# 32 expert slots shared by two requests, with experts 8 to 31 loaded in the order of a list sorted on the chip

## What is computed

```python
g_idx = argmax(h @ rg_w + rg_b)                       # one of 4 groups of 8 experts
e_sel = (h @ re_w + re_b) of that group               # 8 logits
top_p, top_i = lax.top_k(softmax(e_sel), 2)           # two experts of the group per token
top_w = g_w * top_p / sum(top_p)
hid = silu(h @ w_gate[e]) * (h @ w_up[e]); hid *= combine
y   = sum over e of hid @ w_down[e]
x   = layer_norm(alpha * x + g2 * y)
```

## Time and profile before

| | |
|---|---|
| median of 3 runs | 1063.39 us (1060.44 to 1066.7) |
| span of the profiled execution | 1059.0 us; the page gives no other time for this execution |
| TensorE matmul busy | 957.8 us, 90% of the span |
| VectorE, ScalarE, GpSimd busy | 323.2, 230.0, 36.1 us |
| transfers | 324.60 MB, mean 307 GB/s |
| mean granted TensorE clock | 0.977 of 2.4 GHz |

### The profile page before, as it was taken

One profiled execution on the slowest core, in us unless ns is written; L12 is line 12 of the kernel. 1 busy time (PEld: TensorE's weight loads), 2 busy tenths in 40 slices (PEclk: granted clock), 3 DMA queues, 4 the chain that ended last, 5 costly groups with the idle time before them and its releaser, 6 DMA issues.

```text
span 1059.0 us, 15641 instructions
## 1 busy us (share of the span) xinstructions
PE 957.8 (90%) x6820; PEld 584.3 (55%) x6820; DVE 323.2 (31%) x744; ACT 230.0 (22%) x475; POOL 36.1 (3%) x54
## 2 busy tenths in 40 slices
PE   4999899998998999987979998999998999999695
PEld 1787758776843434324338886687885343432431
DVE  2112323122662212112171232331266331211216
ACT  2102313300143213111131032241014321211111
POOL 0200000010001000000010000000000200000000
PEclk9899999999999999998989999999999999999898
DMA  9948864496658999999798206766466699999981
GB/s 381 409 164 320 361 234 174 170 313 274 282 195 360 399 431 428 430 421 425 299 374 348 108 34 244 306 273 215 162 252 258 273 432 427 427 432 425 424 329 51
DMA packets 38526, 324.60 MB, mean 307 GB/s; under 512 B 4920, under 2 KB 5048, under 8 KB 9392
## 3 DMA queue, kind: packets, MB, share of 16 engines
q1 hardware_dynamic: 34816, 313.02, 72.5%
q0 software_dynamic: 3200, 9.09, 2.7%
q10 hardware_dynamic: 432, 1.39, 0.3%
HBM read 321.05 MB, written 2.42 MB: 305 GB/s over the span
## 4 chain that ended last, share of the span: by engine, by line
PE 83%; ACT 5%; DVE 5%; DMA 4%; issue 3%; SPq 0%; DVEq 0%; ACTq 0%
PE ps L804 16%; PE ps L853 11%; PE ps L699 9%; PE ps L725 6%; PE ps L999 5%; PE ps L913 5%; PE ps L985 5%; PE ps L817 5%; DMA dense<-in_w_ada 4%; PE ps L628 3%; PE ps L863 3%; PE ps L649 2%; PE ps L950 2%; PE ps L669 2%; PE ps L940 2%
## 5 line engine op out<-in xcount | busy, mean ns | idle before, releaser
L804 PE MATMUL ps<-expert_gate_up,gathered_prompt 128*32 128x512 f32 x768 | 170.7, 598 | 4.2 <-ACT gathered_sample L1180 2.3
L804 PE MATMUL ps<-expert_gate_up,gathered_sample 128*32 128x512 f32 x768 | 170.7, 598 | 0.0
L853 PE MATMUL ps<-expert_down,hiddenT 128*32 128x512 f32 x1024 | 118.1, 596 | 9.7 <-ACT gathered_sample L1180 4.6
L699 PE MATMUL ps<-hT,dense 128*128 128x256 f32 x512 | 114.2, 381 | 0.0
L804 PEld LDWEIGHTS ps<-expert_gate_up,gathered_prompt 128*32 128x32 f32 x768 | 48.6, 111 | 114.2 <-issue 111.5
L699 PEld LDWEIGHTS ps<-hT,dense 128*128 128x128 f32 x512 | 96.1, 190 | 15.4 <-issue 2.5
L1595 DVE SCALAR_TENSOR_TENSOR y_lo<-ps,slot_weight,y_hi 128x512 fp32r<-128x512 f32 x64 | 48.1, 751 | 117.3 <-ACT y_hi L1214 117.2
L853 PEld LDWEIGHTS ps<-expert_down,hiddenT 128*32 128x32 f32 x1024 | 31.6, 109 | 76.2 <-issue 59.8
L628 PE MATMUL ps<-dense,cond 128*32 128x256 f32 x768 | 53.2, 406 | 17.0 <-ACT cond L1236 11.7
L725 PE MATMUL ps<-dense,hT 128*128 128x256 f32 (+1 forms) x320 | 66.9, 372 | 1.7 <-ACT hT L1137 1.7
L1578 DVE TENSOR_TENSOR hidden<-hidden,ps 128x256 f32<-128x256 f32 x32 | 13.4, 420 | 179.5 <-ACT hidden L1196 179.4
(11 more groups left out here) (218 smaller groups left out, 1129.4 us busy)
## 6 DMA issues: line engine op xcount, KB each, us to landing
expert_gate_up<-in_w_gu SPq DMA_DIRECT2D x64, 2048.0 KB, 17.2
expert_down<-in_w_dn SPq DMA_DIRECT2D x64, 1024.0 KB, 12.0
dense<-in_w_ada SPq DMA_DIRECT2D x48, 1024.0 KB, 9.1
dense<-in_w_in SPq DMA_DIRECT2D x28, 1024.0 KB, 10.4
dense<-in_w_o SPq DMA_DIRECT2D x8, 1024.0 KB, 6.1
dense<-in_w_out SPq DMA_DIRECT2D x8, 1024.0 KB, 4.9
dense<-in_w_c SPq DMA_DIRECT2D x4, 1024.0 KB, 24.8
dense<-in_w_uq SPq DMA_DIRECT2D x4, 576.0 KB, 6.8
```

The lines of the kernel that those rows point to most:

```text
L699: last = mm(b[:, m * 256:(m + 1) * 256], w[:, k, m * P:(m + 1) * P], hT[:, k, :], start=(k == 0), stop=(k == KD - 1))
L804: last = mm(ps[r0:r0 + 32, q, :], xg[s][:, k, at_:at_ + CAP], w_gu[BUFFER[i * EPI + 2 * q + j]][:, k, :], start=(k == 0), stop=(k == KD - ...
L853: last = mm(ps[32 * e:32 * e + 32, banks[c], :], h, w_dn[BUFFER[i * EPI + e]][:, f, c * 512:(c + 1) * 512], start=(f == 0), stop=(f == 1), ...
```

## The change

Both requests share 32 slots per expert. The sample's tokens take the places after the prompt's (`tot0`, `ahead`). The tokens are modulated before the gather, not after it: `turn_tokens` transposes the router's `h2T` back, ScalarE copies the high half (`token_high`) and VectorE the low one (`token_low`), so the gather adds both requests in one PSUM tile and the evacuation is a copy.

There are nine groups instead of eight passes of two requests: experts 0 to 7 in two groups of four; then two groups (2 and 3) of two experts with 64 slots each; then five groups of four. Which experts stand at places 8 to 31 is decided on the chip: `sort_experts` ranks experts 8 to 31 by their tokens of both requests, with ties broken by number, and writes their numbers to `order`. SP reads them into registers, four at a time, and takes the source address of each load from the register. `by_load` reorders positions and weights. The rounds are counted with 64 slots for the four fullest.

The diff, cut to its core:

```diff
+FIXED = 2 * EPI
+FREE = NE - FIXED
 CHUNK = 2 * EPI * CAP
-MAX_ROUNDS = P // CAP
-SPLIT_AT = ITERS - 2
+MAX_ROUNDS = 2 * P // CAP
+
+
+GROUPS = 9
+SPLIT = 7
+FIRST_OF = (0, 4, 8, 10, 12, 16, 20, 24, 28)
+CHUNK_OF = (0, 0, 1, 1, 2, 2, 3, 3, 4)
+COLUMN_OF = (0, 128, 0, 128, 0, 128, 0, 128, 0)
+CHUNKS = 5
+GROUPS_OF = ((0, 1), (2, 3), (4, 5), (6, 7), (8,))
+PLACES_OF = ((0, 8), (8, 12), (12, 20), (20, 28), (28, 32))
+WIDE = 1
+PAIRS = (2, 3)
 ALPHA = float((2 * DEPTH) ** 0.25)
...
+            def main_load(l, e, which=None):
+
+                sp.wait_ge(*reached(M[l], "h_filled", group_of(before_in(e)) + 1))
+                gate_up_load(l, M[l], e, which)
+
+            def main_down(l, e, which=None):
+
+                sp.wait_ge(*reached(M[l], "y_filled", 2 * group_of(before_in(e)) + 2))
+                down_load(l, M[l], e, which)
+
+            def four_experts(l, a):
+
+                with ExitStack() as hold:
+                    which = [whose(hold, e) for e in range(a, a + EPI)]
+                    for g in range(group_of(a), group_of(a + EPI - 1) + 1):
+                        for e in sorted(set(tiles(g))):
+                            main_load(l, e, which[e - a])
+                        for e in sorted(set(tiles(g))):
+                            main_down(l, e, which[e - a])
 
             def extra_loads(l, r):
...
                 first_gate_up(l, 4)
                 first_down(l, 4)
-                k, v = nth(l, ("route", 1))
+                k, v = nth(l, ("tokens", 1))
                 sp.wait_ge(filled[k], v + 1)
                 down_load(l, M[l], 5)
...
+                for e in (6, 7):
                     main_load(l, e)
...
+                for e in (6, 7):
                     main_down(l, e)
+                sp.wait_ge(order_ready, l + 1)
+                for a in range(FIXED, FIRST_OF[SPLIT + 1], EPI):
+                    four_experts(l, a)
                 sp.wait_ge(rounds_ready, l + 1)
...
+                four_experts(l, FIRST_OF[SPLIT + 1])
...
+            def expert(name, l, e, which):
+
+                if e < FIXED:
+                    return io[name][l, e]
+                return io[name][l, bass.ds(which, 1)].rearrange("e p a b -> (e p) a b")
+
...
+            def whose(hold, e):
+
+                if e < FIXED:
+                    return None
+                r = hold.enter_context(sp.register(f"expert_number{len(numbers)}"))
+                numbers.append(e)
+                sp.reg_load(r, order[0:1, e - FIXED:e - FIXED + 1])
+                return sp.snap(r, min_val=FIXED, max_val=NE - 1)
...
+            def gather_first(w, s):
+
+                for f in range(4):
+                    for k in (2 * f, 2 * f + 1):
                         for hp, part in enumerate((h_hi, h_lo)):
+                            at_ = k % 2 * CHUNK
+                            last = mm(ps[:, FIRST_BANK[f], at_:at_ + CHUNK], part[:, s, k * P:(k + 1) * P],
+                                      sel[:, 0, s, :], start=(s == 0 and k % 2 == 0 and hp == 0), stop=True,
+                                      skip_group_check=True)
+                    if s:
+                        last.then_inc(w["xg_filled"], 1)
+
...
+            def gate_up(w, r, g, bank):
+
+                held, n, at_ = tiles(g), CHUNK_OF[g], COLUMN_OF[g]
+                for e in sorted(set(held)):
                     pe.wait_ge(*reached(w, "gu_in", landed(r, e), BUFFER[e]))
                 for k in range(KD):
+                    for j in range(EPI):
+                        last = mm(ps[32 * j:32 * j + 32, bank, :], xg[n % 2][:, k, at_ + j * CAP:at_ + (j + 1) * CAP],
+                                  w_gu[BUFFER[held[j]]][:, k, :], start=(k == 0), stop=(k == KD - 1),
+                                  skip_group_check=True)
                 last.then_inc(w["h_filled"], 1)
...
+                pe.wait_ge(out_drained, 8 * l + 6)
+                turn_tokens(l, 0)
                 ada(l, a0)
                 ada(l, a0 + 1)
+                turn_hidden2(l, 1)
                 count(l, 0)
                 ada(l, a0 + 2)
+                router(l, 1)
+                turn_tokens(l, 1)
+                ada(l, a0 + 3)
+
+                pe.wait_ge(out_drained, 8 * (l + 1))
                 pe.wait_ge(*reached(m, "sel_ready", 1))
+                pe.wait_ge(lo_ready, 4 * l + 2)
+                gather_first(m, 0)
                 count(l, 1)
                 pe.wait_ge(*reached(m, "sel_ready", 2))
+                pe.wait_ge(lo_ready, 4 * l + 4)
+                gather_first(m, 1)
                 evacuated(l, ("count", 0), ("count", 1))
+
+                for g in range(GROUPS):
+                    n = CHUNK_OF[g]
+                    if g:
+                        pe.wait_ge(*reached(m, "selT_copied", g + 1))
+                    gathered(m, 2 * n + 2)
+                    gate_up(m, None, g, g % 2)
+                    if g == 0:
+                        pe.wait_ge(comb_ready, 2 * l + 2)
+                        select_T(m, 0, 2)
+                    elif g <= SPLIT:
+                        scatter(m, g - 1, g - 1, g == 1)
+                    if g == GROUPS_OF[n][-1] and g < SPLIT:
+                        pe.wait_ge(*reached(m, "sel_ready", n + 3))
+                        if n == 0:
+                            pe.wait_ge(sorted_ready, l + 1)
+                        gather(m, n + 1, (2, 3, (g + 1) % 2, 2), 2 * n + 2)
+                        gathered(m, 2 * n + 4)
+                    turn_group(m, g, g, g % 2)
+                    if g < SPLIT:
+                        select_T(m, g + 1, (g + 1) % 2)
+                    if g == 0:
+                        pe.wait_ge(*reached(m, "selT_copied", 1))
+                    down(m, None, g, g)
+                    if g == 0:
+                        if l == 0:
+                            turn(7)
+                        pe.wait_ge(ada_biased, 8 if l == 0 else 12)
+                        if l == 0:
+                            pe.wait_ge(cols_ready, 6)
+                    if g == SPLIT:
+                        scatter(m, g, g, False)
                         pe.wait_ge(rounds_ready, l + 1)
                         r_more = pe.value_load(rounds[0:1, 0:1], min_val=0, max_val=MAX_ROUNDS - 1)
                         with pe.If(r_more > 0):
                             with pe.Fori(0, r_more) as r:
                                 extra_round(l, r)
                             tr(ps[:, 0, 0:P], ident, ident).then_inc(X[l]["done"], 1)
+                        pe.wait_ge(*reached(m, "sel_ready", CHUNKS + 1))
+                        select_T(m, g + 1, 0)
+                        gather(m, n + 1, (2, 3, 1, 2), 2 * n + 2)
+                scatter(m, GROUPS - 1, GROUPS - 1, False)
...
+            def token_high(l, s):
+
+                for c in range(2):
+                    if s == 0:
+                        act.wait_ge(tokens_filled, 2 * l + c + 1)
+                        b = ps[:, TOKEN_BANK[c], :]
+                    else:
+                        b, _ = take(l, ("tokens", c))
+                    actf(h_hi[:, s, c * 512:(c + 1) * 512], b, ACT.Copy).then_inc(hi_ready, 1)
+
...
+            def sort_experts(l):
+
+                grid = [P, FREE, FREE]
+                number = const[:, C_SLOT:C_SLOT + FREE]
+                evacuated(l, ("count", 1))
+                link(V.scalar_tensor_tensor(key[:, :], total[:, FIXED:NE], 64.0, number, ALU.mult, ALU.subtract))
+                link(V.tensor_tensor(sort[:, :, :], key[:, :].unsqueeze(1).to_broadcast(grid),
+                                     key[:, :].unsqueeze(2).to_broadcast(grid), ALU.is_ge))
+                link(V.tensor_reduce(nth_[:, :], sort[:, :, :], AX.X, ALU.add))
+                link(V.tensor_tensor(sort[:, :, :], nth_[:, :].unsqueeze(1).to_broadcast(grid),
+                                     number.unsqueeze(2).to_broadcast(grid), ALU.is_equal))
+                names = const[:, C_SLOT + FIXED - 1:C_SLOT + NE - 1]
+                link(V.tensor_tensor(product[:, 0, :, :], sort[:, :, :], names.unsqueeze(1).to_broadcast(grid), ALU.mult))
+                link(V.tensor_reduce(load[:, :], product[:, 0, :, :], AX.X, ALU.add))
+                V.tensor_copy(order[:, :], load[:, :]).then_inc(order_ready, 1)
+                dve.wait_ge(order_ready, l + 1)
+
+            def by_load(src, dst):
+
+                grid = [P, 2, FREE, FREE]
+                link(V.tensor_tensor(product[:, :, :, :], sort[:, :, :].unsqueeze(1).to_broadcast(grid),
+                                     src[:, :, FIXED:NE].unsqueeze(2).to_broadcast(grid), ALU.mult))
+                return V.tensor_reduce(dst[:, :, :], product[:, :, :, :], AX.X, ALU.add)
...
                 e = mean(1, 4, 5, LN_EPS)
                 centre(t_res, ln1, 1)
                 scale(e, ln1, 1, 5, x1_ready, l)
                 e = row_sums(x, 1, 7, LN_EPS)
                 prepare(e, 1, 7)
+                choose(l, 0)
                 hidden2(l, 1)
```

(61 more changed lines are left out.)

641 lines of the change are left out of this document (232 added, 409 removed).

## The result

Four runs of the changed kernel gave 1048.7 to 1051.3 us, a median of 1050.2; the kernel before, in the same comparison, 1061.9. The ratio is 0.988 with an interval of 0.985 to 0.990: faster by 1.2%, 11.7 us, where 27 were forecast. The span of the profiled execution is 1049.2 us against 1059.0.

What follows compares the result with a forecast made beforehand. The prediction took the transfer ring to become the sole bound of the expert stage. Gains of 14 us in layer 0 and 13 in layer 1, 27 in all, took 1063.4 to 1036 us; range 1026 to 1058.

Steps and rivals of the forecast that it cites:

- the two bounds: Expert stage: TensorE and the transfer ring both full; removing nearly 150 us of TensorE work leaves the ring the bound alone.
- The 183 us for the ring: Each layer's expert loads, 77.6 MB from group 0's gate-up to the last gate-up weights: 180.5 to 184.8 us, taken as 183.
- 201 was forecast: From the end of group 0's gate-up to the residual: 201 us after the change, 214.1 before in layer 0.
- The register reads: SP's 24 reads per layer for load addresses: between nothing and 25 us per layer, taken as zero under queued loads.
- The rival of the starved ring: Each register read stops SP with the ring dry: up to 25 us per layer, 1087 us; chance 0.08.
- no further round: Against the rival that shared slots overflow and a round loads 100.7 MB again, 234 us; chance 0.01.
- group 8: Last expert group of a layer: starts some 3 us after its weights with a warm clock, making TensorE's and ring paths equal.
- a tail: From the last gate-up weights to the residual: gate-up after idling 9.8 us, silu to residual 8.2, and 0.1 before it.
- the stage before group 0: From the last output matmul to group 0's gate-up end: gain 0.5 us per layer, bounds -3 and +2.
- Two such places give 2.6 us back: Before group 0, TensorE's waits for x_hat (4 us) and the sample's low (3 us) slow later work by 2.6 us.
- The rule: Every expert group would start cold after DMA waits; the sum has one cold gate-up on the path at each layer's end.
- The rival of the cold path: Matmul bursts stay at low clock in last gate-up, down, scatters and router: some 10 us per layer, 1056 us; chance 0.13.

Runs made afterwards that it cites:

- e8: The kernel before with half of every expert's bytes loaded and the matmuls reading them twice: 1060.5 us, ratio 0.999 to the kernel before.
- e9: The changed kernel with half of every expert's bytes loaded and the matmuls reading them twice: 955.5 us, ratio 0.898 to the kernel before.
- e2: The changed kernel without the check of the rounds and the further round on four engines: 1039.6 us, ratio 0.979 to the kernel before.
- e5: The changed kernel with the check kept but its loop's body cut to one instruction on each of four engines: 1042.2 us, ratio 0.980 to the kernel before.
- e1: The changed kernel with all expert loads from fixed addresses, no register reads for them, the wait for the list kept: 1050.5 us, ratio 0.988 to the kernel before.
- e4: The changed kernel with eight needless matmuls where TensorE waits for the sample's x_hat in each layer: 1043.1 us, ratio 0.982 to the kernel before.
- e0: The changed kernel run once more, unaltered: 1052.1 us, ratio 0.990 to the kernel before.
- e3: The changed kernel with the check of the rounds moved from behind group 7 to behind group 5: 1044.8 us, ratio 0.985 to the kernel before.
- e6: e3 with group 7's scatter placed ahead of group 8's gate-up: 1040.8 us, ratio 0.980 to the kernel before.
- e7: e6 with needless matmuls in three waits of each layer (8, 10 and 20): 1034.2 us, ratio 0.973 to the kernel before.

## Why the prediction was right, and where it was wrong

The direction was right and the size was not.

**Right: the two bounds.** "Taking work from one exposes the other" is e8 and e9. The 183 us for the ring from group 0 to the last gate-up weights measured 185.0 (e2, e5), and the steady 430 GB/s were 429. With the check out of the way `res` is 202.4 where 201 was forecast. The register reads were costed at nothing and cost nothing (e1), and the list was ready 6.6 us behind the last copy of chunk 0 (317.5 to 324.1), where 7.0 were forecast. The rival of the starved ring is gone with that, and no further round ran.

**Wrong: group 8.** The step that failed is "the check of the rounds costs 6.3 us of silence and the transposes and gather behind it about 6, so group 8 may start some 3 us after its weights but with a warm clock, which makes both paths equal". It took the silence and the gather from the earlier trace rows, 12.3 us together, and had TensorE warm behind them. Measured in layer 0 were 5.4 us of silence, 3.2 more in the gather, and the gather at half clock: 17.8 us from scatter to gate-up. In layer 1, with one silence, it was 13.5. Group 8 started 6.9 and 2.7 us after the ring's time, and its gate-up took 9.3 and 9.8 us: late and cold, where the forecast had either the one or the other. In layer 1 the "some 3 us" were right and the warm clock wrong; in layer 0 both were wrong. e2 priced the whole at 9.8 us for the two layers, e5 showed that the length of the skipped code makes the silences. That is the largest part of the miss; the remaining 2.7 of the 12.5 us that the two stretches to the residual and the end took too long are the ring's 2 us per layer (185.0 for 183), less a tail of 17.4 us from there to the residual where 18.1 were forecast. (The 9.8 in that tail should be 9.6 by its own terms, 7.1 and half of 4.9.)

**Mis-sized: the stage before group 0.** "Two such places give 2.6 us back" priced a silence by the nearest row's 1.8 us. Two of these are 3.6, not 2.6, and would have made the stage 0.6 us longer, not 0.5 shorter. One silence of 3.87 us cost 3.0 (e4), since half clock lasted from 297.5, where the silence ends, to 309.9. In layer 0 the stage grew by 1.6 where it was to shrink by 0.5; in layer 1 the forecast held. Both lie in the stated bounds, 3 us shorter to 2 longer. In e5's profile, where the clock was low behind both silences, the same stage took 39.9 us: outside them.

**Not in the sum: 3.0 us in the dense stage of layer 0**, which the change leaves almost as it was. Programs that are alike in this stage ended it anywhere from 284.6 to 289.1 us, with 6.8 to 17.1 us at the low clock. A forecast against one profile can't have it; a range can.

**The rule.** The Trainium skill ("TensorE: Matmul & The Clock Gate", section "HAM oscillation — how this bites in real kernels") says that waits for DMA between bursts of matmuls bring the low clock back each time. The trace agrees: in the changed kernel gate-ups behind such waits (3.4 to 14.4 us long) took 8.4 to 9.9 us where 7.07 is full clock. It doesn't make every group start cold, as the prediction read it: groups 2 and 3, which had no wait, took 7.08. Beside the ring the cold ones cost nothing, as the prediction had it (g0 is 185.0 in both layers of e2 and e5).

The low clock also came where the wait was not for DMA: behind the wait for x_hat and behind the check. These lie on the path, and there the prediction had one cold gate-up per layer; its own case in the earlier trace rows was such a wait too. The rival of the cold path, 1056 us, is nearer to the result than the forecast, but by luck: it wanted a last gate-up of 14.2 us, cold from end to end, and 4 us more in the down matmuls and scatters behind it. Measured were 9.3 and 9.8, and a tail 0.7 us shorter than forecast. Only its 1 to 2 us for the router stage came, in layer 0.

**Chances.** Faster, 0.84, was right, and the range of 1026 to 1058 held the 1050, in part since it reached to that rival; the forecast itself was 14 us low.

## What to carry to other kernels

When an engine stops being the bound, its path doesn't leave the sum: follow it once more at the end of each stage, where the hidden work comes out, with every silence priced as its own length plus the half-clock time behind it. A check that jumps over much code belongs where the engine has slack, not before the last group: behind group 5 even an 11 us silence cost nothing visible. A wait that can't be shortened may be filled where the work behind it is on the path: here 3.7 us of needless matmuls gave 3.0 us back.

## What the runs showed of the hardware

- Jumping over the long body of a loop that isn't run left TensorE silent for 4.9 to 5.7 us in the full-size kernels, and in one of the two layers again for 1.8 to 3.2 us some matmuls later (in layer 0 of the changed kernel, e0, e1, e3 and e6, in layer 1 of e4). In e7 one silence was 11.0 us, and in e9 one was 6.6. With a body of one instruction there was no silence (e5). A 16 KB packet of an instruction queue fell inside each of the changed kernel's silences.
- After 3.87 us without work TensorE ran at 1.2 GHz (granted clock 0.50) for some 12 us, though it was busy throughout; filling that wait kept the clock up (e4). A silence of 2.66 us left the clock up in the changed kernel, and one of 2.67 was followed by 6.8 us at the low clock in e4. Ten matmuls of filling with 3.4 us of wait behind them didn't keep the clock up for the next group (e7: gate-up 8.8 us).
- One and the same stretch of code was run with 6.8 to 17.1 us at the low clock and took 284.6 to 289.1 us, the longer the more.
- A load whose address is in a register ran at the same 429 GB/s as one with a fixed address; a register read on SP took 0.46 us.
